# A streaming encoder layer: the first 128 rows of expert 0 as a step of their own inside the routing gap

## The reference

```python
g_idx = jnp.argmax(p_grp, axis=-1)                      # top-1 of 4 groups
top_v, top_i = lax.top_k(e_logits, TOP_K_INNER)         # top-2 of the group's 4 experts
top_w = jax.nn.softmax(top_v, axis=-1) * g_gate
expert_id = g_idx[:, None] * EXPERTS_PER_GROUP + top_i
h = silu(x @ w1[e]) * (x @ w3[e]) * gates[..., e]       # 16 experts, 1024 -> 256
y = sum over e of h @ w2[e]                             # 256 -> 1024
x = layer_norm(ALPHA * x + y)
```

## Time and profile before

| | us |
|---|---|
| median of 3 runs | 1265.47 |
| lowest and highest | 1263.98 to 1266.08 |
| profiled execution | 1268.18 |
| its span, first to last instruction | 1266.5 |
| TensorE busy | 1152.0 (91%) |
| VectorE busy | 791.1 (62%) |
| ScalarE busy | 538.9 (43%) |
| POOL busy | 175.3 (14%) |

### The profile page before, as it was taken

One profiled execution on the slowest core, in us unless ns is written; L12 is line 12 of the kernel. 1 busy time (PEld: TensorE's weight loads), 2 busy tenths in 40 slices (PEclk: granted clock), 3 DMA queues, 4 the chain that ended last, 5 costly groups with the idle time before them and its releaser, 6 DMA issues. The chain is left out here.

```text
span 1266.5 us, 20946 instructions
## 1 busy us (share of the span) xinstructions
PE 1152.0 (91%) x5826; PEld 1030.0 (81%) x5827; DVE 791.1 (62%) x1511; ACT 538.9 (43%) x689; POOL 175.3 (14%) x189
## 2 busy tenths in 40 slices
PE   6999999999999999999999776779998999999980
PEld 6999999999999999788888665558886877787760
DVE  5666554654464466466666467445754798787775
ACT  4465443453363364122322123334644666656430
POOL 1000000000010001022222233040000132212232
PEclk9999999999999999999999887879999999999995
DMA  5332679558837425344332226726766789878564
GB/s 186 122 91 79 135 99 105 103 132 104 114 95 281 171 80 169 130 147 151 134 133 100 88 99 247 259 80 235 268 240 262 254 297 364 297 272 293 206 209 150
DMA packets 87131, 221.07 MB, mean 175 GB/s; under 512 B 19136, under 2 KB 45792, under 8 KB 80800
## 3 DMA queue, kind: packets, MB, share of 16 engines
q1 hardware_dynamic: 58544, 131.47, 30.6%
q0 software_dynamic: 18160, 59.53, 13.8%
q10 hardware_dynamic: 10368, 29.37, 12.0%
HBM read 134.80 MB, written 85.53 MB: 174 GB/s over the span
## 5 line engine op out<-in xcount | busy, mean ns | idle before, releaser
L1367 PE MATMUL ps_h<-w_hi,xt_hi 128*128 x336 | 135.9, 404 | 0.7 <-issue 0.7
L1367 PE MATMUL ps_h<-w_lo,xt_hi 128*128 x336 | 131.8, 392 | 0.0
L1367 PE MATMUL ps_h<-w_hi,xt_lo 128*128 x336 | 131.6, 392 | 0.0
L284 PE MATMUL ps_vb_c<-x_hi,w_hi 128*128 (+1 forms) x320 | 114.5, 358 | 11.2 <-DVE x_lo L453 11.1
L284 PE MATMUL ps_vb_c<-x_hi,w_lo 128*128 (+1 forms) x320 | 113.7, 355 | 0.0
L284 PE MATMUL ps_vb_c<-x_lo,w_hi 128*128 (+1 forms) x320 | 113.0, 353 | 0.0
L284 PE MATMUL ps_va_b<-x_hi,w_lo 128*128 (+1 forms) x320 | 112.7, 352 | 0.0
L284 PE MATMUL ps_va_b<-x_hi,w_hi 128*128 (+1 forms) x320 | 112.6, 352 | 0.0
L284 PE MATMUL ps_va_b<-x_lo,w_hi 128*128 (+1 forms) x320 | 111.8, 349 | 0.0
L1030 DVE TENSOR_TENSOR w_lo<-w_raw,w_hi 128x2048 f32 (+1 forms) x32 | 73.1, 2286 | 15.7 <-ACT w_hi L1025 15.3
L1367 PEld LDWEIGHTS ps_h<-w_hi,xt_lo 128*128 128x128 f32 x336 | 63.6, 189 | 13.8
(11 more groups left out here) (333 smaller groups left out, 2682.2 us busy)
## 6 DMA issues: line engine op xcount, KB each, us to landing
w_raw<-in_w SPq DMA_DIRECT2D x48, 1024.0 KB
w_lo_p<-xs_scr SPq DMA_DIRECT2D x43, 512.0 KB
o_scr<-w_lo_p SPq DMA_DIRECT2D x42, 512.0 KB
o_scr<-x_raw ACTq DMA_DIRECT2D x40, 512.0 KB, 7.8
w_raw<-in_w_in POOLq DMA_DIRECT2D x19, 512.0 KB, 3.6
x_raw<-in_x_t SPq DMA_DIRECT2D x20, 416.0 KB, 3.4
xs_scr<-x_raw ACTq DMA_DIRECT2D x16, 512.0 KB, 8.0
x_hi_p<-y_scr SPq DMA_DIRECT2D x16, 512.0 KB, 4.3
```

The source lines that it names most:

```text
L284: mm = pe.matmul(ps[i][:, 0:CHUNK], w[:, i, k], x[:, k, bass.ds(c * CHUNK, CHUNK)], start=(k == 0 and n == 0), stop=(k == KT - 1 and n == 2))
L1367: mm = pe.matmul(ps_h[par][:], x[:, par, k], w[:, bass.ds(at, 1), k].rearrange("p o n -> p (o n)"), start=(k == 0 and n == 0), stop=(k == ...
```

## The change

- **Reserved rows.** After the last group that block 1 scatters, `reserve` moves the start of expert 0's region in VectorE's books by 128 (and the running count to at least 128). The first 128 slots become step 0, which needs no plan. All pairs shift by one: step 0 alone, then (1, 2), (3, 4) and so on; the number of steps is odd.
- **Step 0.** SyncE waits at the end of block 1 for the scatters of tiles 0 to 13, and loads the first 128 rows of `xs_scr` and `g_scr` first in block 2. TensorE turns them before the plan's matmuls; its step 0 stands ahead of the wait for the plan. The filler matmuls are gone; the ranking counts follow step 0's up-projection. ScalarE loads silu's table in the gap.
- **Ranking.** `ranks` moves behind `x_lo(1)` in step 0, `slots` into step 2, `records` into step 3, `count_pairs` into step 5.
- **Records.** The 17 scatters go out in steps 4 to 6, as groups of 2, 3, 3, 3, 3, 3, each behind VectorE's `x_lo` or hidden rows of that step.
- **Zero fills.** Four more, ahead of the mixer's second group, for the second 128 rows of expert 0's region and two more blocks of `o_scr`.

Seven steps (0 to 6) are unrolled in place of six. The core of the diff:

```diff
-STEPS = (TOPK * TOK + NE * P) // P
+STEPS = 1 + (TOPK * TOK + NE * P) // P
...
-STORED, OFILL = 8, 8
-PLAN = 2 * ((STEPS - NT) // 2 + 1 + FTAIL)
+STORED, OFILL = 7, 8
+PLAN = 2 * ((STEPS - NT) // 2 + FTAIL)
+FILLS = 2 + 2 * NE + STEPS - STORED
...
+        act.wait_ge(s_zero, 1)
+        act.dma_start(xs_scr[P:2 * P, :], zero).then_inc(s_zo, 16)
+        act.dma_start(g_scr[P:2 * P, :], zero[:, 0:1]).then_inc(s_zo, 16)
+        for i in range(STORED + (NCH - 2) * OFILL, STEPS - NE):
+            act.dma_start(o_scr[i * P:(i + 1) * P, :], zero).then_inc(s_zo, 16)
...
+    def reserve(self, dve, n):
+        dve.wait_ge(self.s_read, n + 1)
+        dve.memset(self.start[:, 0:1], float(P))
+        self.then(dve, dve.tensor_scalar(self.run[:, 0:1], self.run[:, 0:1], float(P), None, ALU.max))
...
+            for n in range(LAST - 5, LAST - 1):
+                sp.wait_ge(rt.s_sc[n % 4], rt.landed(n))
+            sp.wait_ge(rt.s_gs, 16 * TOPK * GROUPED[LAST - 1][0])
...
                 for n in ends_at(t - 2):
                     rt.places(dve, n, ps_c)
+                    if n == LAST - 2:
+                        rt.reserve(dve, n)
...
+            emit(0, 0, 0, 3, None)
             eng.wait_ge(s_plan, 1)
-            for s in range(6):
-                emit(s, s % 2, s // 2, 2, None)
+            for s in range(1, 7):
+                emit(s, s % 2, s // 2, 3, None)
             eng.wait_ge(s_pairs, 1)
             pairs = eng.value_load(planned[0:1, 0:1], min_val=0, max_val=PLAN // 2 - FTAIL - 3) + (FTAIL + 3)
             with eng.Fori(3, PLAN // 2 - FTAIL) as h:
                 with eng.If(h < pairs - FTAIL):
-                    emit(h * 2, 0, h, 2, None)
-                    emit(h * 2 + 1, 1, h, 2, None)
+                    emit(h * 2 + 1, 1, h, 3, None)
+                    emit(h * 2 + 2, 0, h + 1, 3, None)
...
+                emit(pairs * 2 - (2 * FLAST - 1 - n), (n + 1) % 2, pairs - (FLAST - (n + 1) // 2), min(3, 2 * FLAST - 1 - n),
                      (last_tile(f + 1), last_tile(f), last_tile(f - 1)))
-            return pairs * 2 - 1, pairs - 1
+            return pairs * 2, pairs
...
+            sp.dma_start(xg[:, 0], xs_scr[0:P, :]).then_inc(s_xg[0], 16)
             sp.dma_start(consts[:, 0:NCONST], consts_in).then_inc(s_con, 16)
+            sp.dma_start(gate[:, slot(0, 0)], g_scr[0:P, :]).then_inc(s_g[0], 16)
             for half in (0, 1, None):
                 load_weights(sp, 0, half)
             sp.dma_start(ln2[:], ln[:, 2:4]).then_inc(s_ln2, 16)
             sp.wait_ge(s_plan, 1)
-            for n in range(LAST - 3, LAST + 1):
+            for n in (LAST - 1, LAST):
                 sp.wait_ge(rt.s_sc[n % 4], rt.landed(n))
-            ahead = [load(s, s) for s in range(2)]
+            ahead = [load(1, 1), load(2, 0)]
             sp.wait_ge(rt.s_gs, 16 * TOPK * NT)
-            for s in range(2):
-                load_gate(s, s, 0, ahead[s])
-            load_gate(2, 0, 1, load(2, 0))
+            load_gate(1, 1, 0, ahead[0])
+            load_gate(2, 0, 1, ahead[1])
...
-                if isinstance(s, int) and s == 2:
-                    pool.wait_ge(s_rec, 1)
-                    for t in range(NT):
-                        pool.indirect_dma_start(fin_scr, bass.IndirectOffsetOnAxis(fint[:, 3, t:t + 1], 0),
-                                                rec[:, t], None).then_inc(s_put, 16)
+                if isinstance(s, int) and 4 <= s < 7:
+                    if s == 4:
+                        pool.wait_ge(s_rec, 1)
+                    for half, done in enumerate((s_xlo, s_hid)):
+                        pool.wait_ge(done, s + (2 - half))
+                        n = (s - 4) * 2 + half
+                        for t in range(NT * n // 6, NT * (n + 1) // 6):
+                            pool.indirect_dma_start(fin_scr, bass.IndirectOffsetOnAxis(fint[:, 3, t:t + 1], 0),
+                                                    rec[:, t], None).then_inc(s_put, 16)
...
+            def count_later():
+                pe.wait_ge(s_later, 1)
+                of = later.rearrange("p t e -> p (t e)")
+                pe.matmul(ps_o[1][:, 0:NT * NE], consts[:, C_TRI:C_TRI + P], of, start=True, stop=True)
+                pe.matmul(ps_o[0][:, 0:NT * NE], consts[:, C_ONE:C_ONE + P], of, start=True, stop=True).then_inc(s_cnt2, 1)
             def step(s, par, h, left, tiles):
-                if isinstance(s, int) and s == 3:
+                if isinstance(s, int) and s == 5:
                     pe.wait_ge(s_need, 1)
                     pe.matmul(ps_c[0:1, 384:512], need[:], consts[:, C_ID:C_ID + P], start=True, stop=True).then_inc(s_row, 1)
-                expert = pe.value_load(plan[0:1, 0, bass.ds(s, 1)], min_val=0, max_val=NE - 1)
+                expert = 0 if early(s, 1) else pe.value_load(plan[0:1, 0, bass.ds(s, 1)], min_val=0, max_val=NE - 1)
                 at = expert % 2
-                if left:
+                if left and not early(s, 1):
                     turn(s + 1, 1 - par, h if par == 0 else h + 1)
                 pe.wait_ge(s_xlo, s + 1)
                 pe.wait_ge(s_13lo, expert * 2 + 2)
@@ -1367,15 +1398,21 @@
                         mm = pe.matmul(ps_h[par][:], x[:, par, k], w[:, bass.ds(at, 1), k].rearrange("p o n -> p (o n)"),
                                        start=(k == 0 and n == 0), stop=(k == KT - 1 and n == 2))
                 mm.then_inc(s_h, 1)
-                if not early(s, 1):
+                if early(s, 1):
+                    count_later()
+                else:
                     output(s - 1, pe.value_load(plan[0:1, 0, bass.ds(s - 1, 1)], min_val=0, max_val=NE - 1))
                 pe.wait_ge(s_hid, s + 1)
                 for k in range(FT):
                     mm = pe.transpose(ps_ht[:, k], hid[:, k * P:(k + 1) * P], consts[:, C_ID:C_ID + P])
                 mm.then_inc(s_th, 1)
+                if early(s, 1):
+                    turn(1, 1, 0)
...
+            turn(0, 0, 0)
             pe.wait_ge(s_vals, 1)
             pe.wait_ge(rt.s_read, LAST + 1)
@@ -1383,15 +1420,6 @@
                 mm = pe.matmul(ps_c[0:1, 128 + i * (PLAN + 1):128 + (i + 1) * (PLAN + 1)], vals[:, i:i + 1],
                                consts[:, C_ID:C_ID + PLAN + 1], start=True, stop=True)
             mm.then_inc(s_pp, 1)
-
-            pe.wait_ge(s_later, 1)
-            of = later.rearrange("p t e -> p (t e)")
-            pe.matmul(ps_o[1][:, 0:NT * NE], consts[:, C_TRI:C_TRI + P], of, start=True, stop=True)
-            pe.matmul(ps_o[0][:, 0:NT * NE], consts[:, C_ONE:C_ONE + P], of, start=True, stop=True).then_inc(s_cnt2, 1)
-
-            for i in range(40):
-                pe.matmul(ps_h[1][:, 0:P], consts[:, C_ID:C_ID + P], consts[:, C_ID:C_ID + P], start=True, stop=True)
-            turn(0, 0, 0)
...
+                if early(s, 1):
+                    act.wait_ge(s_h, 1)
+                    act.activation(sil[:], ps_h[0][:, 0:FE], ACT.Silu).then_inc(s_sil, 1)
+                    x_hi(1, 1)
+                    residual(1, 1, 0)
+                    act.wait_ge(s_sil, 1)
+                    return
...
+            act.wait_ge(rt.s_exp, LAST + 1)
+            act.activation(idle[:], rt.gex[:, 0, 0:1], ACT.Silu)
+            x_hi(0, 0)
+            residual(0, 0, 0)
             ew.hi13(act, 0, first)
             ew.hi2(act, 0, first)
-            x_hi(0, 0)
-            residual(0, 0, 0)
...
+            def hidden(s, par, h):
+                dve.wait_ge(s_sil, s + 1)
+                dve.wait_ge(s_th, s)
+                dve.wait_ge(s_g[par], h * 16 + 16)
+                dve.scalar_tensor_tensor(out=hid[:], in0=sil[:], scalar=gate[:, slot(par, h)],
+                                         in1=ps_h[par][:, FE:2 * FE], op0=ALU.mult, op1=ALU.mult).then_inc(s_hid, 1)
...
+                if early(s, 1):
+                    hidden(0, 0, 0)
+                    x_lo(1, 1)
+                    ranks()
+                    dve.wait_ge(s_hid, 1)
+                    return
...
-                if isinstance(s, int) and s == 1:
+                if isinstance(s, int) and s == 2:
+                    slots()
+                if isinstance(s, int) and s == 3:
                     records()
-                if isinstance(s, int) and s == 3:
+                if isinstance(s, int) and s == 5:
                     count_pairs()
...
-            later_experts()
+            x_lo(0, 0)
             ew.lo13(dve, 0, first)
             ew.lo2(dve, 0, first)
-            ranks()
-            slots()
-            x_lo(0, 0)
+            later_experts()
             dve.memset(mv[:], 0.0)
```

More of the change, by code:

```diff
@@ L1137, in pair @@
             def pair(tile, h, more):
[L1138 to L1139 removed]
+                emit(h * 2 + 1, 1, h, 3, (None, None, tile(-1)) if more else None)
+                emit(h * 2 + 2, 0, h + 1, 3, (tile(1), tile(0), None))
             h = pairs - FTAIL
[L1142 to L1143 removed]
+            emit(h * 2 + 1, 1, h, 3, None)
```

(56 more changed lines are left out.)

41 lines of the change are left out of this document (16 added, 25 removed).

## The result

The changed kernel took 1252.18 us (median of 4 executions, 1248.49 to 1254.29) beside 1264.76 us for the kernel before (median of four: the three executions of the table of the time before, and one more): 12.6 us less, a ratio of 0.9896 (95% interval 0.9870 to 0.9922). Forecast were 1234.3 us and a range of 1226 to 1246. The direction was right; 18 us of the gain are missing. The profiled execution took 1251.43 us (span 1249.7).

A forecast was written before the change was run, and what follows sets the result against it. TensorE, busy 91% of the span, was taken to bound the kernel, so only removed matmuls or closed holes pay. Gain 36.4 less 4 (scatters), 0.7 (exit) and 0.5 (final tiles) is 31.2 us: 1234.3 us, range 1226 to 1246.

The forecast's parts named there:

- Steps saved: Expert step loop: 42 steps become 41 because the padding step goes, worth 9.27 us.
- The opening: Start of block 2: step 1's first up-projection matmul comes at 788.5 us instead of 804.44, worth 15.9 us.
- Ranking, slots and records moved: Steps 0 to 3: VectorE's later queue makes TensorE wait 2.4 us for h_lo(3); bound 0 to 5 us.
- The scatters: Steps 4 to 6: of the 12.7 us stall beside 17 scatters, grouping leaves 4 us, bounds 0 to 12.7.
- Small terms: Loop exit 0.7 us, final-tile parity 0.5, extra zero fills 0 (at most 2), slot-reserving instructions 0.
- the parity flips: Final-tile phase: ScalarE's roots and table loads meet weight splits in five more steps, costing 0.5 us, ends -2 and 3.
- The exit: End of the step loop: TensorE passes a ninth empty turn, costing 0.7 us more issue.
- Sum: Whole kernel: 36.4 - 4 - 0.7 - 0.5 = 31.2 us gained, giving 1234.3 us.
- (a): Record scatters: the stall keeps its whole 12.7 us instead of 4, giving 1243.0 us; chance 0.19.
- (b): Opening: loads hold it, expert 1's weights landing 8 us later, giving 1242 us; chance 0.10.
- (c): Scatter groups: every group stalls code supply by itself, 41 us in all, giving 1271.3 us; chance 0.05.

The follow-up runs named there:

- e5: Changed kernel with the records written in step 2, right behind the slots, instead of step 3: 1253.81 us, ratio 0.9977.
- c1: Changed kernel, unchanged, run again in another set: 1256.80 us, ratio 0.9997 to the kernel before.
- e4: Changed kernel with all 17 record scatters in one run in step 4 instead of six groups: 1257.69 us, ratio 1.0004.
- h1: Changed kernel, unchanged, run once more in a later set: 1250.46 us, ratio 0.9960 to the kernel before.
- h2: Changed kernel with all 17 scatters in one run in step 4, repeated in a later set: 1250.57 us, ratio 0.9963.
- g1: Kernel before, unchanged, run and profiled once more in another set: 1271.17 us, ratio 0.9994.
- g2: Kernel before with only its 17 scatters spread in six groups over steps 2 to 4, repeated in another set: 1260.51 us, ratio 0.9917.
- e3: Kernel before with only its 17 scatters spread in six groups over steps 2 to 4: 1258.55 us, ratio 1.0016.
- e6: Changed kernel with final-tile fetch and sum on each pair's first step and records in step 2: 1246.03 us, ratio 0.9915.
- e1: Changed kernel with final-tile fetch and sum back on each pair's first step, norm on the second: 1246.61 us, ratio 0.9911.
- e2: Kernel before with its final tiles moved one step on, to the changed kernel's pairing: 1261.46 us, ratio 1.0039.
- g3: Changed kernel with all 17 scatters in one run in step 4, repeated in another set: 1270.93 us, ratio 1.0002.
- c2: Kernel before, unchanged, run again for a second profile: 1258.33 us, ratio 1.0002.
- g4: Changed kernel with final-tile fetch and sum on each pair's first step and records in step 2, repeated in another set: 1253.46 us, ratio 0.9876.

## Why the prediction was wrong

**Steps saved** was right: 41 stores, and two steps more cost 15.7 us by the clock.

**The opening** was right in its end, h(1) at 788.66 for 788.5, but by luck: block 2 started 2.4 us earlier than before, at 753.56, and from there to h(1) it took 35.1 us, not the 32.5 forecast. Thirteen matmuls of h(0) ran at the low clock, not ten, and the turn of step 1's rows was followed by a 2.46 us wait for x_lo(1), so that the turn of step 2 and the start of h(1) ran at the low clock (0.77 us for a first matmul, 0.63 for the next, against 0.48 and 0.39). The prediction has a low clock at h(0) alone. h(2) came 11.3 us behind h(1), not 10.4.

**Ranking, slots and records moved** failed by size: 2.4 us of TensorE's wait for h_lo(3), inside a bound of 0 to 5. The wait was 3.65 us, it dropped the clock (1.05 us for two matmuls, 0.62 at full clock), and h(5) came 15.3 us behind h(4), not 11.8. The slots, costed at nothing, had a price too: they (809.70 to 812.70 us) and 2.42 us of issue stand ahead of h_lo(2) at 815.11, TensorE waits 1.01 us for it and 0.28 for hid(3), and h(4) came 11.6 behind h(3), not 9.4. With the 0.9 of h(2) that is the 6.6 us between the forecast h(5), 829.5, and the measured 836.18. e5 says that taking records out of step 3 doesn't take this away: the work then stands in front of h_lo(2).

**The scatters** were costed on a stall that is real but not everywhere. On chip A the profile before has it and the profile after has a small rest of it: behind ScalarE's "remote" wait of 2.63 us the silu of step 6 comes 11.4 us after that of step 5, and TensorE loses the time in the next step, with the 1.61 us "issue" row. 3.3 us are lost in nine steps (forecast 4), but c1, e4, h1 and h2, without a stall, lose 0.8 to 1.1 there too, so the scatters' part is about 2.3. The prediction read the stall as "issue" of all engines at once; g1 shows ScalarE held, TensorE slowed and VectorE behind ScalarE. g2 shows what the grouping is worth on a chip with the stall, 9.8 us (12.7 less 4 was forecast: 8.7). On B it is worth nothing (e3), nor on F (h1 and h2); on F the change gains 4.2 us and on C 0.6, which is within the noise, not the 12.6 to 16.8 of A and D. This step of the sum was right for the chip of the result, and wrong as a statement on the kernel: one execution was taken for all.

**Small terms** failed, and this is the largest part: "the parity flips ... 0.5, ends -2 and 3". The stretch grew by 9.5 us. Moving the tiles back takes 9.2 (e6 against c1) to 10.6 us (e1 against e4) off it, and 7.8 (e6 against e5) to 11.1 us (e1 against e4) off the time. I had counted one collision (a root on ScalarE meeting a weight split) and no other; the trace shows that TensorE's waits for hid and for the rows and ScalarE's wait for the weights are all longer in this placing. The wait for the weights is the one that comes with the placing in both kernels (e2); which of the three leads was not separated, and no run moves the loads alone. The exit cost 6.38 us of issue for 5.60, 0.8 as forecast (0.7):

```profile
931.92 6.38 issue
```

**Sum.** 31.2 less 6.3 (opening and queue), 9.0 (placing), 1.0 (exit), plus 0.7 and 1.2 is 16.8 between the profiled executions, and 3.5 of frame make 13.3; against 1264.76, the median of before with its fourth execution, it is 12.6. Counted from the start of block 2, the first term is 2.4 larger, and block 1 gave that back. **The rivals**: none had this. (a) and (b) end at 1243.0 and 1242 by other mechanisms; (c), every group stalling by itself at full size, is refuted by g2 and h1. The interval of the range was built from the steps that looked uncertain, and the 9 us came from one that I had declared small after counting only one of its collisions.

## What to carry to other kernels

When a change shifts a schedule by one step, everything that is laid on odd and even steps must be priced again, or moved back with it: here that was worth 8 to 11 us, where the change itself gained 12.6 to 16.8 on A and D, 4.2 on F and nothing that can be told on C, and a few lines undo the loss. A hole in one profiled execution is a fact of that execution; before it is put into a sum, look at a second profile, on another chip if there is one. And work moved out of the shadow of a wait needs a place with room on its engine: moved by one step, the queue moves with it.

## What the runs showed of the hardware

- One run of 17 indirect scatters (1.26 us apart) goes with a stall of 11 to 13 us in the profiles of two sets (before, g1, g3) and with none in those of three others (e2, e4, c2, h2), with the same code. In the stall TensorE starts a matmul of 0.4 us every 2.1 us, ScalarE stands for 12 us, VectorE behind it, POOL goes on, and the DMA share is 0.13 (g1). Groups of two and three with waits between them shorten it: the interval is 11.9 us in g2 for 23.2 in g1, and ScalarE's "remote" wait 1.6 for 12.1. That the scatters hold up the supply of instructions is argued from "issue" alone; no run shows it, nor why the sets differ. The two queues that the profile calls instruction queues move one block each at this place in g1 (829 and 831 us) and in c2 (826 and 829), so they don't tell the two apart.
- The Trainium skill (Runtime: NRT & Kernel Launch, Instruction fetch mechanics) has straight code prefetched with its cost mostly hidden. The trace of c2 agrees: none of its first six intervals is over 10.3 us. If the stall is one of instruction supply, which no run shows, g1 and g3 don't agree, by 13 and 11 us.
- The profiled execution can lie far from the timed ones of the same kernel and chip: c1 1245.70 against a median of 1256.80, g4 1246.91 against 1253.46. c1 and c2 are 17.4 us apart in their profiled executions and 1.5 in their medians. So a comparison of two profiles can be off by more than 15 us in the whole, and is of use only stretch by stretch.
